# First mixer: one sink addition and one reciprocal for both steps of a pair, statistics side by side

## The chip, the cores and the metric

The kernel runs on one core of one Trainium2 chip. The metric is the device time of one execution in microseconds (us), taken as the median of repeated runs.

## The reference

The kernel computes two transformer blocks on 256 tokens of width 1024, in float32. The first block is a mixer followed by a mixture of experts with 32 experts; the second has a pooling and latent-attention mixer, a recurrent mixer, two cross-attentions and two gated feed-forward layers. The change touches only the attention of the first mixer. It has two kinds of heads: 24 dilated heads in three groups of eight, whose three groups are merged by a softmax over their log-sums, and 16 sliding-window heads with a sink.

```
# dilated: per group, then merged over the three groups
scores = q.k * hd**-0.5 + bias;  m = max;  p = exp(scores - m);  denom = sum(p)
out = (p @ v) / denom;  lse = m + log(denom)
alpha = softmax(lses over the 3 groups);  y = sum(alpha * outs)
# sliding window, with a sink per head
m = maximum(max(scores), sink);  p = exp(scores - m)
denom = sum(p) + exp(sink - m);  out = (p @ v) / denom
```

Merging three softmaxes by their log-sums equals one softmax over the three groups' scores side by side, and the kernel computes it so.

## The kernel before

The tokens are two blocks of 128. All weights come in units of 1 MB (128 partitions x 2048 elements); ScalarE makes the rounded high part of a unit (`whi`, L1653) and VectorE the remainder (`wlo`, L2337), and TensorE multiplies with high and low parts three times over. The DMAs of the units are issued by SyncE as buffers come free.

The attention of the first mixer has 32 steps (`steps_a`). Steps 0 to 15 are dilated (`dil`): one head index, one block of queries, the scores of the three groups side by side, so that a step has 3 x 128 scores per query for the first block and 3 x 256 for the second. Steps 16 to 31 are sliding-window (`swa`): two heads at a time, 2 x 128 or 2 x 256 scores. Steps are handled in 16 pairs; this document calls them pair 0 to pair 15. In the dilated part, pairs 0, 2, 4, 6 are two steps of 128 keys and pairs 1, 3, 5, 7 two steps of 256 keys. In the sink part (pairs 8 to 15) the first step of a pair has 128 keys, the second 256.

What each engine does, in the order of its program (`attend_two` of each):

- TensorE, for pair p: the scores of pair p+1 (`score_two`, L914), the transposes of the first step's probabilities (`turn`, L864), a quarter of a gate unit of the projection (`fourth_unit`, 12 matmuls, L701 to L703), the transposes of the second step, another quarter, then probabilities times values of both steps (`mix_two`, L937). The second `turn` waits until ScalarE has copied the first step's transposes out of PSUM.
- ScalarE: copies the transposes of both steps (`copy_turned`, L1766 and, for six blocks, L1769), then exponentials with their sums for both steps of the next pair (`exps`: L1751 dilated; L1747 for the two sinks and L1755 twice in the sink part). The sum arrives with the row called ACTIVATION_READ_ACCUMULATOR. After the exponentials of some pairs it makes a `whi` (L1653) or copies a finished gate unit out (L1724).
- VectorE: `probs` of the first step, `probs` of the second, the copy of a finished output (L2573), then for the next pair twice `bias_max` (the biased scores, L2500; their maximum, L2505 or L2508; with sinks L2510; the negated maximum, L2513 or L2515). After every odd pair's `bias_max` of the next pair it has one `wlo` to make (L2337), or at two places a shorter operation.

`probs` waits for the step's exponentials (`att_exp`), adds the sink's exponential to the sum (L2523, sink part only), takes the reciprocal (L2524) and scales the probabilities (L2526 for a dilated step, L2534 twice for a sink step). The small operations are chained: `link` puts a semaphore increment on one and makes VectorE wait for it before the next.

The scores lie in three buffers `S[s % 3]` of the scratch `scr`, the statistics of a step in the row `s % 3` of `sm` (columns 0 to 2 maxima, 3 to 5 negated, 6 to 8 sums, 9 to 11 reciprocals, 12 to 14 sinks' exponentials).

Of the kernel before, what the change touches and what calls it, by code (L numbers as in the profile page):

```python
# [24 lines left out]
ALU = mybir.AluOpType  # L25
ACT = mybir.ActivationFunctionType
AX = mybir.AxisListType
# [90 lines left out]
def build(nc, t, out):  # L118

    with ExitStack() as ctx:  # L120
# [28 lines left out]
        sm = sb("sm", [P, 3, 24])  # L149
# [73 lines left out]
        def tok_of(part):  # L223
# [39 lines left out]
        att_scored, att_biased, att_max, att_exp, att_probs = (sem("att_scored"), sem("att_biased"), sem("att_max"),  # L263
                                                               sem("att_exp"), sem("att_probs"))
# [129 lines left out]
        def score_bank(step, g):  # L394

            if step["kind"] == "dil":
                bank, at = 5 * step["head"], g * T
                if step["nk"] == P:
                    bank, at = step["head"], g * P
                elif g == 2:  # L400
                    bank, at = 1, step["head"] * T
            else:
                bank, at = g, step["qt"] * T if step["kind"] == "swa" else 0
                if step["kind"] in ("xa", "mla"):
                    bank, at = step["qt"], g * step["nk"]
            return ps[:, bank, at:at + step["nk"]]

        def gather_bank(c, low):

# [81 lines left out]
        S = [scr[:, b * 768:(b + 1) * 768].rearrange("p (g k) -> p g k", g=3) for b in range(3)]  # L491
# [16 lines left out]
        steps_a = attention("dil") + attention("swa")  # L508
# [1134 lines left out]
        def _(act):  # L1643
# [96 lines left out]

            def exps(s, step):
                act.wait_ge(att_max, s + 1)
                b, nk = s % 3, step["nk"]
                n = len(step["scores"])
                if step["sink"] is not None:
                    for g in range(2):
                        nc.scalar.activation(sm[:, b, 12 + g:13 + g],  # L1747
                                             sink_row[:, step["sink"] + g:step["sink"] + g + 1],
                                             ACT.Exp, bias=sm[:, b, 3 + g:4 + g])
                if step["merged"]:  # L1750
                    last = nc.scalar.activation(S[b][:, 0:n, 0:nk], S[b][:, 0:n, 0:nk], ACT.Exp,  # L1751
                                                bias=sm[:, b, 3:4], scale=step["scale"], accum_out=sm[:, b, 6:7])
                else:
                    for g in range(n):
                        last = nc.scalar.activation(S[b][:, g, 0:nk], S[b][:, g, 0:nk], ACT.Exp,  # L1755
                                                    bias=sm[:, b, 3 + g:4 + g], scale=step["scale"],
                                                    accum_out=sm[:, b, 6 + g:7 + g])
                last.then_inc(att_exp, 1)

            def copy_turned(s, step, PT):  # L1760
# [274 lines left out]
            for k, u in enumerate(u_br):  # L2035
                for half in range(2):
                    act.wait_ge(sg_scaled, 2 * k + half + 1)
                    two = sg[:, 8 * half + 2 * k:8 * half + 2 * k + 2, :]
# [9 lines left out]
            for c in range(DC):  # L2048
                last = nc.scalar.activation(xg[:, c, :], x[:, c, :], ACT.Copy, scale=vcol("g_ffn", c))
# [11 lines left out]
            for b in range(4):  # L2061
                last = nc.scalar.activation(tok_of(xh)[:, b, :, :], ps[:, b, :].rearrange("p (q k) -> p k q", k=4),
                                            ACT.Copy, scale=rcol[:, b // 2:b // 2 + 1])
# [10 lines left out]
            for b in range(2):  # L2074
                last = nc.scalar.activation(mem_sq[:, 4 * b:4 * b + 4, :], mem[:, 4 * b:4 * b + 4, :], ACT.Square)
# [245 lines left out]
        def _(dve):  # L2321
# [3 lines left out]
            def link(ins):  # L2325

                st["chain"] += 1
                ins.then_inc(dve_step, 1)
                dve.wait_ge(dve_step, st["chain"])
# [154 lines left out]
            def bias_max(s, step):  # L2484
                dve.wait_ge(att_scored, s + 1)
                if s >= 3:
                    dve.wait_ge(att_turned, s - 2)
                b, nk, n = s % 3, step["nk"], len(step["scores"])
                for g in range(n):
                    src = score_bank(step, g)  # L2490
                    dst = S[b][:, g, 0:nk]
                    if step.get("by_key"):
                        last = v.tensor_tensor(dst, src, mem_rstd, ALU.mult)
                    elif step["bias"] is None:
                        last = v.tensor_copy(dst, src)
                    elif step["bias"] == "causal":
                        last = v.tensor_tensor(dst, src, causal[:, T - nk:T], ALU.add)
                    else:
                        pi, slope = step["bias"][g]
                        last = v.scalar_tensor_tensor(out=dst, in0=pat[:, pi, T - nk:T], scalar=-slope, in1=src,  # L2500
                                                      op0=ALU.mult, op1=ALU.add)
                last.then_inc(att_biased, 1)
                dve.wait_ge(att_biased, s + 1)
                if step["merged"]:
                    link(v.tensor_reduce(sm[:, b, 0:1], S[b][:, 0:n, 0:nk], AX.XY, ALU.max))  # L2505
                    n = 1
                else:
                    link(v.tensor_reduce(sm[:, b, 0:n], S[b][:, 0:n, 0:nk], AX.X, ALU.max))  # L2508
                if step["sink"] is not None:
                    link(v.scalar_tensor_tensor(out=sm[:, b, 0:n], in0=sm[:, b, 0:n], scalar=step["scale"],  # L2510
                                                in1=sink_row[:, step["sink"]:step["sink"] + n],
                                                op0=ALU.mult, op1=ALU.max))
                    v.tensor_scalar(sm[:, b, 3:3 + n], sm[:, b, 0:n], -1.0, None, ALU.mult).then_inc(att_max, 1)  # L2513
                else:
                    v.tensor_scalar(sm[:, b, 3:3 + n], sm[:, b, 0:n], -step["scale"], None,  # L2515
                                    ALU.mult).then_inc(att_max, 1)

            def probs(s, step):
                dve.wait_ge(att_exp, s + 1)
                b, nk, n = s % 3, step["nk"], len(step["scores"])  # L2520
                k = 1 if step["merged"] else n
                if step["sink"] is not None:
                    link(v.tensor_tensor(sm[:, b, 6:6 + k], sm[:, b, 6:6 + k], sm[:, b, 12:12 + k], ALU.add))  # L2523
                link(v.reciprocal(sm[:, b, 9:9 + k], sm[:, b, 6:6 + k]))  # L2524
                if step["merged"]:
                    last = v.tensor_scalar(S[b][:, 0:n, 0:nk], S[b][:, 0:n, 0:nk], sm[:, b, 9:10], None, ALU.mult)  # L2526
                else:
                    for g in range(n):
                        if step.get("by_key"):
                            last = v.scalar_tensor_tensor(out=S[b][:, g, 0:nk], in0=S[b][:, g, 0:nk],  # L2530
                                                          scalar=sm[:, b, 9 + g:10 + g], in1=mem_rstd,
                                                          op0=ALU.mult, op1=ALU.mult)
                        else:
                            last = v.tensor_scalar(S[b][:, g, 0:nk], S[b][:, g, 0:nk], sm[:, b, 9 + g:10 + g], None,  # L2534
                                                   ALU.mult)
                last.then_inc(att_probs, 1)

            def attend(steps, y_of, between=None):
                base = st["step"]
# [27 lines left out]
            def attend_two(y_of, between):  # L2567
                n = len(steps_a)

                def out(s):  # L2570
                    if steps_a[s]["last"]:
                        dve.wait_ge(att_mixed, s + 1)
                        v.tensor_copy(y_of(st["y"], 1)[:, 0, :], ps[:, 4, 0:T]).then_inc(att_out, 1)  # L2573
                        st["y"] += 1

                bias_max(0, steps_a[0])
                bias_max(1, steps_a[1])
                for s in range(0, n, 2):
                    probs(s, steps_a[s])
                    probs(s + 1, steps_a[s + 1])  # L2580
                    if s:
                        out(s - 1)
                    if s + 2 < n:
                        bias_max(s + 2, steps_a[s + 2])
                        bias_max(s + 3, steps_a[s + 3])
                    between(s)
                    between(s + 1)
                out(n - 1)
                dve.wait_ge(att_out, st["y"])
                st["step"] += n  # L2590
# [850 lines left out]
```

## Time and profile before

| what | us |
|---|---|
| median of 3 runs (lowest to highest) | 1705.93 (1705.73 to 1707.23) |
| the profiled execution, its own time | 1706.17 |
| its span, first to last instruction | 1704.3 |
| TensorE matmul busy | 1635.1 (96%) |
| VectorE busy | 1328.5 (78%) |
| ScalarE busy | 1032.5 (61%) |
| attention of the first mixer | about 152 to 262 |

The busy shares are means over stages with different limits. An engine's rows come from one execution: each has a start and a duration, and in brackets the time the engine stood idle just before it and whose work ended that. The time of 1706.17 us contains the span and 1.87 us around it. A busy TensorE is not a TensorE at its peak, since the ends of matmuls are modelled.

### The profile page before, as it was taken

The numbers are of one execution on the slowest core, as the hardware profiler recorded it, in microseconds if no ns is written. First come the engines' busy times: TensorE is split into PE (matmuls) and PEld (weight loads), VectorE is DVE, ScalarE is ACT, GpSimd is POOL, SyncE is SP. The second block draws the span as 40 slices with busy tenths as digits, with TensorE's granted clock in tenths as the row PEclk, the third lists the DMA queues.
The fourth block names the chain that finished last, engine by engine and source line by source line (L and its number), as shares of the span: only waits on it lengthen the run. The fifth ranks groups of instructions, "written<-read, shape, count | busy, mean of one in ns | idle before, by whom it ended". The sixth has DMA issues, their size and how long they took to land.

```text
span 1704.3 us, 27827 instructions
## 1 busy us (share of the span) xinstructions
PE 1635.1 (96%) x10558; PEld 1429.4 (84%) x10558; DVE 1328.5 (78%) x1510; ACT 1032.5 (61%) x1137; POOL 60.8 (4%) x57
## 2 busy tenths in 40 slices
PE   8999989899999999999998988999999999999998
PEld 7998879778877667777776978999999999998887
DVE  6545897674589999999996987778767879677776
ACT  4333676454678999999986564454435394454443
POOL 0000000000000000000004230000000020000000
PEclk9998999999999999999999999999999999999999
DMA  9663124085799999999999443446554565445550
GB/s 324 195 191 100 54 72 152 9 321 182 256 370 422 422 423 422 423 422 423 423 418 336 135 151 110 138 149 222 187 183 150 172 199 181 140 139 196 192 177 25
DMA packets 186397, 392.21 MB, mean 230 GB/s; under 512 B 6976, under 2 KB 151104, under 8 KB 161728
## 3 DMA queue, kind: packets, MB, share of 16 engines
q1 hardware_dynamic: 184496, 383.89, 61.6%
q0 software_dynamic: 1808, 7.05, 1.1%
q8 instruction: 63, 1.03, 0.2%
q14 instruction: 30, 0.25, 0.0%
HBM read 380.29 MB, written 10.62 MB: 229 GB/s over the span
## 4 chain that ended last, share of the span: by engine, by line
PE 64%; DMA 13%; DVE 13%; issue 5%; ACT 4%; POOL 0%; SPq 0%; DVEq 0%; ACTq 0%; POOLq 0%
DMA raw<-w_e_up_dram 11%; PE ps L969 9%; DVE wlo L2337 6%; PE ps L683 5%; PE ps L688 5%; PE ps L684 5%; PE ps L975 5%; PE ps L1155 4%; PE ps L984 4%; PE ps L1104 3%; PE ps L1110 3%; PE ps L1106 2%; PE ps L777 1%; PE ps L773 1%; PE ps L771 1%
## 5 line engine op out<-in xcount | busy, mean ns | idle before, releaser
L2337 DVE TENSOR_TENSOR wlo<-raw,whi 128x2048 fp32r<-128x2048 f32 (+3 forms) x358 | 811.3, 2278 | 165.5 <-ACT whi L1653 157.2
L1653 ACT ACTIVATE whi<-raw 128x2048 fp32r<-128x2048 f32 (+3 forms) x358 | 675.7, 1891 | 301.8 <-PE ps L975 113.6
L683 PE MATMUL ps<-xh,whi 128*128 128x256 f32 x688 | 169.9, 287 | 3.2 <-DVE xl L2350 2.0
L684 PE MATMUL ps<-xl,whi 128*128 128x256 f32 x688 | 167.5, 283 | 0.0
L1104 PE MATMUL ps<-whi,xh 128*128 128x512 f32 x528 | 160.2, 396 | 0.0
L969 PE MATMUL ps<-xb,whi 128*128 128x512 f32 x672 | 160.2, 390 | 0.0
L1110 PE MATMUL ps<-wlo,xh 128*128 128x512 f32 x528 | 143.6, 396 | 2.6 <-DVE wlo L2337 2.4
L969 PEld LDWEIGHTS ps<-xb,whi 128*128 128x128 f32 x672 | 124.0, 188 | 24.4
L683 PEld LDWEIGHTS ps<-xh,whi 128*128 128x128 f32 x688 | 132.3, 192 | 4.3 <-issue 1.8
L684 PEld LDWEIGHTS ps<-xl,whi 128*128 128x128 f32 x688 | 132.3, 192 | 0.3
L1110 PEld LDWEIGHTS ps<-wlo,xh 128*128 128x128 f32 x528 | 97.0, 188 | 31.9 <-DVE wlo L2337 12.2
L1104 PEld LDWEIGHTS ps<-whi,xh 128*128 128x128 f32 x528 | 97.4, 188 | 20.4
L688 PE MATMUL ps<-xh,wlo 128*128 128x256 f32 x688 | 90.0, 283 | 0.0
L975 PEld LDWEIGHTS ps<-xb,wlo 128*128 128x128 f32 x672 | 86.2, 191 | 3.3
L975 PE MATMUL ps<-xb,wlo 128*128 128x256 f32 x672 | 87.2, 283 | 0.0
L688 PEld LDWEIGHTS ps<-xh,wlo 128*128 128x128 f32 x688 | 85.9, 192 | 0.0
L1155 PE MATMUL ps<-whi,ah 128*64 128x512 f32 (+1 forms) x280 | 74.9, 393 | 6.1 <-issue 2.8
L1155 PE MATMUL ps<-wlo,ah 128*64 128x512 f32 (+1 forms) x280 | 76.0, 397 | 2.1 <-DVE wlo L2337 0.3
L1155 PE MATMUL ps<-whi,al 128*64 128x512 f32 (+1 forms) x280 | 74.6, 392 | 0.0
L1155 PEld LDWEIGHTS ps<-wlo,ah 128*64 128x64 f32 (+1 forms) x280 | 39.9, 150 | 31.6 <-DVE wlo L2337 14.0
L1155 PEld LDWEIGHTS ps<-whi,ah 128*64 128x64 f32 (+1 forms) x280 | 41.3, 149 | 28.8 <-issue 7.4
L1681 ACT ACTIVATE xb<-x,vec 128x256 fp32r<-128x256 f32 x40 | 18.2, 502 | 70.5 <-DVE x L2469 70.5
(491 smaller groups left out, 3078.0 us busy)
## 6 DMA issues: line engine op xcount, KB each, us to landing
raw<-w_e_gate_dram SPq DMA_DIRECT2D x64, 1024.0 KB, 10.6
raw<-w_e_up_dram SPq DMA_DIRECT2D x64, 1024.0 KB, 10.5
raw<-w_e_down_dram SPq DMA_DIRECT2D x64, 1024.0 KB, 10.5
raw<-ffn_w_gate_up_dram SPq DMA_DIRECT2D x44, 1024.0 KB, 5.1
raw<-w_in_dram SPq DMA_DIRECT2D x30, 1024.0 KB, 5.5
raw<-ffn_w_down_dram SPq DMA_DIRECT2D x22, 1024.0 KB, 4.8
raw<-xa_w_kv_dram SPq DMA_DIRECT2D x16, 1024.0 KB, 5.5
raw<-xa_w_q_dram SPq DMA_DIRECT2D x8, 1024.0 KB, 5.0
```

The costliest lines, as they stand in the source:

```text
L683: nc.tensor.matmul(o[b], wh, h, start=b == 0 and a == 0, stop=False, skip_group_check=True)
L684: nc.tensor.matmul(o[b], wh, l, start=False, stop=False, skip_group_check=True)
L688: mm = nc.tensor.matmul(o[b], wl, h, start=False, stop=b == len(blocks) - 1 and a == len(parts) - 1, skip_group_check=True)
L969: nc.tensor.matmul(ps[:, bank + b, :], wh[:, k, b * P:b * P + P], xb[:, k, :, :].rearrange("p a t -> p (a t)"), start=k == 0, stop=False, ...
L975: mm = nc.tensor.matmul(ps[:, bank + b, 0:T], wl[:, k, b * P:b * P + P], xb_h[:, k, :], start=False, stop=k == DC - 1, skip_group_check=True)
L984: mm = nc.tensor.matmul(o, part[:, 2 * (j % 2) + k, (bank // 2) * P:(bank // 2) * P + P], weights[:, k, cols], start=begin and n == 0, sto ...
L1104: nc.tensor.matmul(o, h[:, k, :], wh[:, k, :], start=part == 0 and k == 0, stop=False)
L1106: nc.tensor.matmul(o, l[:, k, :], wh[:, k, :], start=False, stop=False)
L1110: mm = nc.tensor.matmul(ps[:, s % 2 + 2 * up, :], rows[s][0][:, k, :], wl[:, k, :], start=False, stop=part == 1 and k == 3)
L1155: mm = nc.tensor.matmul(o, src[s % 2][:, 2 * half + k, 0:w], weights[:, k, cols], start=start and k == 0, stop=stop and k == 1)
L1653: nc.scalar.activation(whi[u % HL][:, 0:n], raw[u % RAW][:, 0:n], ACT.Copy).then_inc(hi_ready, 1)
L2337: v.tensor_tensor(wlo[u % HL][:, 0:n], raw[u % RAW][:, 0:n], whi[u % HL][:, 0:n].bitcast(F32), ALU.subtract).then_inc(lo_ready, 1)
```

## The change

In the 16 pairs, `probs` of the two steps is replaced by `probs_two`, which waits for the exponentials of both steps, then makes one sink addition (sink part) and one reciprocal for both, and then scales the probabilities of the first and of the second step as before. For this the statistics of the two steps must lie in neighbouring rows of `sm`, so for the dilated and sink steps the row is `s % 2` and no longer `s % 3`. The later attentions keep `s % 3` and `probs`. The score buffers stay `S[s % 3]`.

```diff
+        def stat_slot(s, step):
+            return s % 2 if step["kind"] in ("dil", "swa") else s % 3
...
             def exps(s, step):
                 act.wait_ge(att_max, s + 1)
-                b, nk = s % 3, step["nk"]
+                b, nk, st_at = s % 3, step["nk"], stat_slot(s, step)
...
+            def probs_two(s):
+
+                two = steps_a[s:s + 2]
+                n = len(two[0]["scores"])
+                k = 1 if two[0]["merged"] else n
+                dve.wait_ge(att_exp, s + 2)
+                if two[0]["sink"] is not None:
+                    link(v.tensor_tensor(sm[:, 0:2, 6:6 + k], sm[:, 0:2, 6:6 + k], sm[:, 0:2, 12:12 + k], ALU.add))
+                link(v.reciprocal(sm[:, 0:2, 9:9 + k], sm[:, 0:2, 6:6 + k]))
+                for a, step in enumerate(two):
+                    b, nk = (s + a) % 3, step["nk"]
+                    if k == 1:
+                        last = v.tensor_scalar(S[b][:, 0:n, 0:nk], S[b][:, 0:n, 0:nk], sm[:, a, 9:10], None, ALU.mult)
+                    else:
+                        for g in range(n):
+                            last = v.tensor_scalar(S[b][:, g, 0:nk], S[b][:, g, 0:nk], sm[:, a, 9 + g:10 + g], None,
+                                                   ALU.mult)
+                    last.then_inc(att_probs, 1)
...
                 for s in range(0, n, 2):
-                    probs(s, steps_a[s])
-                    probs(s + 1, steps_a[s + 1])
+                    probs_two(s)
                     if s:
                         out(s - 1)
```

In `exps` and `bias_max` every `sm[:, b, ...]` becomes `sm[:, st_at, ...]`; nothing else changes there.

## Rows read from the trace of the kernel before

A "pair" here is the pair of steps whose probabilities or transposes the row belongs to; L1747 rows 215.26, 221.42 and 222.56 open the exponentials of the pair after the one whose transposes were just copied.

**Rows 1.** Page of the whole kernel, the chain that ended last, shares by engine

```profile
PE 64%; DMA 13%; DVE 13%; issue 5%; ACT 4%; POOL 0%; SPq 0%; DVEq 0%; ACTq 0%; POOLq 0%
```

**Rows 2.** VectorE waits in 152 to 262: line waited for, us, times, longest

```profile
DVE sm L2523 <- ACT scr L1755: 2.1, 3, 0.7
```

**Rows 3.** Timeline of VectorE, pairs 5, 6: start us, duration us, instruction [idle before]

```profile
191.75 0.17 DVE L2524 RECIPROCAL sm<-sm 128x1 f32<-128x1 f32 x1 [0.37 <-ACT scr L1751]
191.96 0.62 DVE L2526 TENSOR_SCALAR scr<-scr,sm 128x768 f32<-128x768 f32 x1
192.49 0.68 DVE L2500 SCALAR_TENSOR_TENSOR scr<-c,ps 128x128 f32<-128x128 f32 x3
...
199.70 1.08 DVE L2500 SCALAR_TENSOR_TENSOR scr<-c,ps 128x256 f32<-128x256 f32 x3 [0.65 <-PE ps L914]
```

**Rows 4.** Timeline of ScalarE, pair 5

```profile
191.53 0.19 ACT L1751 ACTIVATION_READ_ACCUMULATOR scr<-scr,sm 128x1 f32 x1
...
193.43 0.57 ACT L1766 ACTIVATE x<-ps 128x512 f32<-128x512 f32 x1
```

**Rows 5.** Timeline of TensorE, pair 5

```profile
191.44 0.87 PE L864 MATMUL ps<-c,scr 128*128 128x128 f32 x6
...
194.42 0.84 PE L864 MATMUL ps<-c,scr 128*128 128x128 f32 x6 [0.68 <-ACT x L1769]
...
196.62 1.53 PE L937 MATMUL ps<-x,arena 128*64 128x128 f32 x24
```

**Rows 6.** Timeline of VectorE, pairs 9 and 10

```profile
218.08 0.16 DVE L2523 TENSOR_TENSOR sm<-sm 128x2 f32<-128x2 f32 x1 [0.67 <-ACT scr L1755]
...
218.48 0.62 DVE L2534 TENSOR_SCALAR scr<-scr,sm 128x256 f32<-128x256 f32 x2
219.01 0.42 DVE L2573 COPY arena<-ps 128x256 f32<-128x256 f32 x1
...
224.57 0.15 DVE L2523 TENSOR_TENSOR sm<-sm 128x2 f32<-128x2 f32 x1
...
224.96 0.48 DVE L2534 TENSOR_SCALAR scr<-scr,sm 128x128 f32<-128x128 f32 x2
225.36 0.15 DVE L2523 TENSOR_TENSOR sm<-sm 128x2 f32<-128x2 f32 x1
```

**Rows 7.** Timeline of ScalarE, pairs 8 to 10

```profile
211.95 0.19 ACT L1755 ACTIVATION_READ_ACCUMULATOR scr<-scr,sm 128x1 f32 x1
...
214.76 0.60 ACT L1766 ACTIVATE x<-ps 128x512 f32<-128x512 f32 x1 [1.47 <-PE ps L864]
215.26 0.47 ACT L1747 ACTIVATE sm<-rows,sm 128x1 f32<-128x1 f32 x2
...
221.42 0.47 ACT L1747 ACTIVATE sm<-rows,sm 128x1 f32<-128x1 f32 x2
...
222.56 0.47 ACT L1747 ACTIVATE sm<-rows,sm 128x1 f32<-128x1 f32 x2
...
223.83 0.19 ACT L1755 ACTIVATION_READ_ACCUMULATOR scr<-scr,sm 128x1 f32 x1
```

**Rows 8.** Timeline of TensorE: pairs 8, 10 and 15

```profile
212.43 0.44 PE L864 MATMUL ps<-c,scr 128*128 128x128 f32 x2
...
214.13 0.60 PE L864 MATMUL ps<-c,scr 128*128 128x128 f32 x4
...
225.50 0.44 PE L864 MATMUL ps<-c,scr 128*128 128x128 f32 x2 [1.52 <-DVE scr L2534]
...
259.03 0.63 PE L864 MATMUL ps<-c,scr 128*128 128x128 f32 x4 [1.01 <-ACT x L1766]
```

**Rows 9.** Stretches in us: length, busy us PE, PEld, DVE, ACT, POOL, PEclk, DMA

```profile
149.75:150.50 0.75, 0.00 (x0) 0.00 (x0) 0.75 (x3) 0.00 (x0) 0.00 (x0) 0.95 0.96 340
156.25:160.50 4.25, 4.24 (x19) 3.23 (x20) 3.13 (x10) 1.26 (x5) 0.00 (x0) 0.50 0.00 0
224.00:225.50 1.50, 0.00 (x0) 0.00 (x1) 1.43 (x6) 0.49 (x2) 0.00 (x0) 1.00 0.00 0
```

More of the change, by code:

```diff
@@ L1746, in exps @@
                     for g in range(2):
-                        nc.scalar.activation(sm[:, b, 12 + g:13 + g],
+                        nc.scalar.activation(sm[:, st_at, 12 + g:13 + g],
                                              sink_row[:, step["sink"] + g:step["sink"] + g + 1],
-                                             ACT.Exp, bias=sm[:, b, 3 + g:4 + g])
+                                             ACT.Exp, bias=sm[:, st_at, 3 + g:4 + g])
                 if step["merged"]:
                     last = nc.scalar.activation(S[b][:, 0:n, 0:nk], S[b][:, 0:n, 0:nk], ACT.Exp,
-                                                bias=sm[:, b, 3:4], scale=step["scale"], accum_out=sm[:, b, 6:7])
+                                                bias=sm[:, st_at, 3:4], scale=step["scale"], accum_out=sm[:, st_at, 6:7])
                 else:
@@ L1755, in exps @@
                         last = nc.scalar.activation(S[b][:, g, 0:nk], S[b][:, g, 0:nk], ACT.Exp,
-                                                    bias=sm[:, b, 3 + g:4 + g], scale=step["scale"],
-                                                    accum_out=sm[:, b, 6 + g:7 + g])
+                                                    bias=sm[:, st_at, 3 + g:4 + g], scale=step["scale"],
+                                                    accum_out=sm[:, st_at, 6 + g:7 + g])
                 last.then_inc(att_exp, 1)
@@ L2488, in bias_max @@
                 b, nk, n = s % 3, step["nk"], len(step["scores"])
+                st_at = stat_slot(s, step)
                 for g in range(n):
@@ L2504, in bias_max @@
                 if step["merged"]:
-                    link(v.tensor_reduce(sm[:, b, 0:1], S[b][:, 0:n, 0:nk], AX.XY, ALU.max))
+                    link(v.tensor_reduce(sm[:, st_at, 0:1], S[b][:, 0:n, 0:nk], AX.XY, ALU.max))
                     n = 1
                 else:
-                    link(v.tensor_reduce(sm[:, b, 0:n], S[b][:, 0:n, 0:nk], AX.X, ALU.max))
+                    link(v.tensor_reduce(sm[:, st_at, 0:n], S[b][:, 0:n, 0:nk], AX.X, ALU.max))
                 if step["sink"] is not None:
-                    link(v.scalar_tensor_tensor(out=sm[:, b, 0:n], in0=sm[:, b, 0:n], scalar=step["scale"],
+                    link(v.scalar_tensor_tensor(out=sm[:, st_at, 0:n], in0=sm[:, st_at, 0:n], scalar=step["scale"],
                                                 in1=sink_row[:, step["sink"]:step["sink"] + n],
                                                 op0=ALU.mult, op1=ALU.max))
-                    v.tensor_scalar(sm[:, b, 3:3 + n], sm[:, b, 0:n], -1.0, None, ALU.mult).then_inc(att_max, 1)
+                    v.tensor_scalar(sm[:, st_at, 3:3 + n], sm[:, st_at, 0:n], -1.0, None, ALU.mult).then_inc(att_max, 1)
                 else:
-                    v.tensor_scalar(sm[:, b, 3:3 + n], sm[:, b, 0:n], -step["scale"], None,
+                    v.tensor_scalar(sm[:, st_at, 3:3 + n], sm[:, st_at, 0:n], -step["scale"], None,
                                     ALU.mult).then_inc(att_max, 1)
```

## Prediction

> **What bounds the kernel now.** I read the page first: of the chain that ended last TensorE has 64%, VectorE and the DMAs 13% each [rows 1]. That is a mean over the whole kernel. The change acts in one stretch, from about 152 to 262 us, so I then read that stretch engine by engine, and of each pair asked which wait ends last.
>
> In the dilated part the answer alternates. In a 256-key pair VectorE gets to the second step's reciprocal before ScalarE has its exponentials ready: it stands idle 0.37 us until 191.75 [rows 3]. The same row is there for pairs 1, 3 and 7. TensorE does not wait for that: it began the first step's transposes at 191.44, before the second step's exponentials were done at 191.53 + 0.19 = 191.72 [rows 4, 5]. What ends last there is ScalarE's copy of the first transposes (from 193.43, held up by a `whi` before it), for which TensorE waits 0.68 us with the second transposes [rows 4, 5]. In a 128-key pair VectorE has finished early and waits 0.65 us for TensorE's scores (199.70) [rows 3]. So in the whole dilated part saved VectorE time is not on the path.
>
> In the sink part VectorE works almost without a gap, and there its time counts; but in pairs 9, 11 and 15 it waits for the second step's exponentials, 2.1 us in all, at most 0.7 [rows 2]. In pair 10 TensorE waits 1.52 us for the first scaled probabilities (225.50) [rows 8].
>
> **The change, edit by edit.** Removed: 16 reciprocals and 8 sink additions of VectorE. Each costs its pitch, not its width: two of them take 218.08 to 218.48, so 0.20 each [rows 6]; a reciprocal in the dilated part 191.75 to 191.96, 0.21 [rows 3]. In sum 24 x 0.20 = 4.8 us of VectorE.
>
> Added: the first step's reciprocal now waits for the second step's exponentials. Queued behind that wait on VectorE are the scaling of the first step, of the second, the output copy and the next pair's biased scores; waiting for the first scaling are TensorE's first transposes and through them ScalarE's copy.
>
> Merged operations: no row shows one over 2 rows of statistics. The low end is the price of one operation (0.20), the high end that of two (0.40). One element and two elements per partition both have a pitch of 0.20 to 0.21 [rows 3, 6], so I take 0.20. 20 of them are on the path found below (4 dilated, 16 sink), so the high end would add 4 us. I give that end little weight; it would need a cost that no row shows for twice the elements.
>
> The row index `s % 2` for `s % 3`: no cost; a row of statistics is rewritten only by `bias_max` behind `probs_two` on the same engine. No DMA is moved, and no queue of SyncE or GpSimd is passed; the loads of weight units follow `wlo` and move with it.
>
> **Pair 0 and the 128-key pairs 2, 4, 6: nothing.** The exponentials of both steps are ready when VectorE comes, it gets 0.2 us earlier to a point where it waits 0.65 us for TensorE [rows 3]. That wait is the cover; nothing is gained or lost.
>
> **The 256-key pairs 1, 3, 5, 7: each a loss.** Let E be the end of the second exponentials, 191.72 in pair 5. Before, the second transposes began at 194.42, E + 2.70 [rows 5]. After: reciprocal at E + 0.03, first scaling 0.21 later, taking 0.62 [rows 3], and about 0.05 to TensorE (the pair-10 gap of 224.96 + 0.48 to 225.50 is 0.06 [rows 6, 8]): first transposes at E + 0.91. Transposes and a quarter unit take 194.42 to 196.62 = 2.20 [rows 5], so the second transposes begin at E + 3.11. The old wait for ScalarE's copy (0.68 us) is covered, since the copy can start almost as early as before. Loss 0.41 each. VectorE leaves the pair at E + 1.31 in place of 192.49 = E + 0.77 [rows 3]; the 0.65 us of wait in the next pair takes that up. From the second transposes on the chain runs through TensorE to the next pair's scores, so nothing gives it back: 4 x 0.41 = 1.64 us.
>
> **Pair 8: a loss.** E is 211.95 + 0.19 = 212.14 [rows 7]. After: addition at 212.18, two pitches of 0.20, scaling 0.48 [rows 6], 0.06 to TensorE: transposes at 213.12 in place of 212.43 [rows 8], 0.69 later, and TensorE is the chain from there.
>
> **Pairs 9 to 15: loss and gain nearly cancel.** Before, from the second transposes of pair 8 (214.13) to those of pair 15 (259.03) are 44.90 us [rows 8]. After, a pair is set by the longer of two loops:
> - through ScalarE: transposes to copy 0.63 (214.13 to 214.76), copy to exponentials 0.50, first step's 1.14 (221.42 to 222.56), second step's 1.46 (222.56 to 223.83 + 0.19) [rows 7, 8]; then 0.03 to VectorE, 0.40, 0.48, 0.06, and first to second transposes 1.70 (212.43 to 214.13) [rows 6, 8]. Sum 6.40.
> - through VectorE, where a `wlo` lies in between: addition and reciprocal 0.40, first scaling's pitch 0.40 (224.96 to 225.36), second scaling to copy 0.53, copy to the next addition 5.56 (219.01 to 224.57) [rows 6]. Sum 6.89. It holds for pairs 10 and 12; in 14 the operations in that place are shorter and the first loop holds.
>
> 5 x 6.40 + 2 x 6.89 = 45.78, against 44.90: loss 0.88. In the first loop VectorE's own release of the second exponentials comes only about 0.1 us sooner than ScalarE, so a small error there does not change it.
>
> Sum: 1.64 + 0.69 + 0.88 = 3.2 us. After 262 us TensorE's work follows at once, then routing, then expert loads that wait for the routing result; all of it moves along. On the profiled execution's 1706.17 this makes 1709.4; on the median of the runs, which is 0.24 lower, 1709.1.
>
> **Rivals.**
> (a) *The saving comes through.* If the second exponentials were always ready when VectorE comes, all 24 pitches would fall off a VectorE-bound path: -4.8 us, 1701.1. For it: the sink part is VectorE-bound, and behind a `wlo` (pair 10) both are ready. It decides from the point where E lies ahead of VectorE's arrival; in pairs 5 and 9 it lies behind it, by waits of 0.37 and 0.67 us even at the second step [rows 3, 6]. Against it also: the 0.65 us waits of the dilated part. This is also what the Trainium skill would have one expect: "VectorE: DVE Perf Modes", section on the TRN2 errata, says that each SBUF-source operation pays a fixed extra latency and that many small tiles should be made into fewer. The trace agrees on the fixed price, but not that it lies on the path.
> (b) *Partly hidden.* ScalarE or TensorE have more slack than the walk gives them, or the lost time is made up where VectorE is last; between -2 and +2.5 us, middle +1: 1706.9.
> (c) *The clock.* TensorE's wait before the last pair's first transposes grows: from the second transposes of pair 14 to there are 6.40 - 1.70 = 4.70 us, of which its work fills 2.20 and about half of a 24-matmul mix of 1.53 [rows 5], leaving some 1.7 us idle. After an idle 0.75 us the granted clock fell near 150 us, and while TensorE was busy from 156.25 it stayed at half (1.2 GHz) for 4.25 us; but 1.5 us of idle at 224 left it at 2.4 GHz [rows 9]. A fall would cost half of 4.25, 2.1 us: 1711.2.
> (d) *The merged operation costs as two:* +4 us more, 1713.1.
>
> **How the numbers follow.** This kernel's runs differ by about 0.1%, and 0.2% (3.4 us) is about what a measurement tells from no change; the forecast of +3.2 lies just inside. Chances: the walk as forecast (+2.5 to +4.2) 0.62, of which 0.36 below 3.4 and 0.26 above; (a) 0.06; (b) 0.15; (c) 0.14; (d) 0.03. Faster 0.06; same 0.36 + 0.15 = 0.51; slower 0.26 + 0.14 + 0.03 = 0.43. The range reaches from the middle of (b) to just past (c): 1706.8 to 1711.6, leaving out (a), (d) and the lower part of (b), less than 2 in 10.
>
> **What would show it.** In the trace of after: the first transposes of 256-key pairs 0.9 us behind the second exponentials' end; the time from one such pair to the next longer by 0.4; the second transposes of pairs 9, 11, 13, 14, 15 at 6.4 us from the ones before; VectorE busy 24 operations less, its idle time more by more than they took; the stretch from 262 us on unchanged in length. Wrong it would be if TensorE's first transposes did not move in pairs 1, 3, 5, 7, or if the merged operations had a pitch well over 0.20.

## The result and the profile after

| what | before | after |
|---|---|---|
| median, us (runs) | 1705.78 (9) | 1711.27 (9) |
| lowest to highest | 1705.03 to 1707.38 | 1704.97 to 1712.99 |
| profiled execution, its own time | 1706.17 | 1710.99 |
| its span | 1704.3 | 1709.1 |
| VectorE busy, instructions | 1328.5, 1510 | 1324.3, 1486 |

The changed kernel takes 1.0028 of the time before (95% interval 1.002 to 1.0036): 4.8 us more by this ratio; the two medians lie 5.5 apart. 24 VectorE instructions and 4.2 us of VectorE work are gone, and the kernel is slower. The predicted 1709.1 lies 2.2 under the median of 1711.27, which is inside the range of 1706.8 to 1711.6.

VectorE's timeline of pairs 5 and 6 after the change (start us, duration us, instruction, idle before it), the answer to [rows 3]:

```profile
193.01 0.17 DVE L2551 RECIPROCAL sm<-sm 128x2 f32<-128x2 f32 x1 [1.09 <-ACT scr L1755]
193.21 1.15 DVE L2555 TENSOR_SCALAR scr<-scr,sm 128x768 f32<-128x768 f32 x2
194.27 0.68 DVE L2505 SCALAR_TENSOR_TENSOR scr<-c,ps 128x128 f32<-128x128 f32 x3
...
201.27 1.08 DVE L2505 SCALAR_TENSOR_TENSOR scr<-c,ps 128x256 f32<-128x256 f32 x3 [0.63 <-PE ps L918]
```

ScalarE and TensorE beside it, for [rows 4, 5]:

```profile
192.79 0.19 ACT L1755 ACTIVATION_READ_ACCUMULATOR scr<-scr,sm 128x1 f32 x1
192.88 1.90 ACT L1657 ACTIVATE whi<-raw 128x2048 fp32r<-128x2048 f32 x1
194.80 0.60 ACT L1770 ACTIVATE x<-ps 128x512 f32<-128x512 f32 x1
```

```profile
193.89 0.87 PE L868 MATMUL ps<-c,scr 128*128 128x128 f32 x6 [1.12 <-DVE scr L2555]
...
196.03 0.82 PE L868 MATMUL ps<-c,scr 128*128 128x128 f32 x6
...
198.20 1.53 PE L941 MATMUL ps<-x,arena 128*64 128x128 f32 x24
```

VectorE's idle time at the reciprocal went from 0.37 to 1.09 us, and TensorE, which before started the first transposes while ScalarE was still at the second exponentials, now waits 1.12 us. The second exponentials end at 192.98; the first transposes start 0.91 after that. The next pair's wait for TensorE (0.65 before, 0.63 now) swallows whatever VectorE saved.

VectorE's timeline of pairs 9 and 10, for [rows 6]:

```profile
220.48 0.16 DVE L2550 TENSOR_TENSOR sm<-sm 128x4 f32<-128x4 f32 x1 [1.64 <-ACT scr L1759]
220.68 0.18 DVE L2551 RECIPROCAL sm<-sm 128x4 f32<-128x4 f32 x1
220.90 1.01 DVE L2558 TENSOR_SCALAR scr<-scr,sm 128x128 f32<-128x128 f32 x4
221.82 0.41 DVE L2597 COPY arena<-ps 128x256 f32<-128x256 f32 x1
...
227.38 0.16 DVE L2550 TENSOR_TENSOR sm<-sm 128x4 f32<-128x4 f32 x1
```

TensorE's transposes of pairs 8, 9 and 15, for [rows 8]:

```profile
215.02 0.44 PE L868 MATMUL ps<-c,scr 128*128 128x128 f32 x2 [0.64 <-DVE scr L2558]
...
216.73 0.60 PE L868 MATMUL ps<-c,scr 128*128 128x128 f32 x4
...
223.13 0.60 PE L868 MATMUL ps<-c,scr 128*128 128x128 f32 x4
```

```profile
260.85 0.44 PE L868 MATMUL ps<-c,scr 128*128 128x128 f32 x2 [1.86 <-DVE scr L2558]
...
262.55 0.60 PE L868 MATMUL ps<-c,scr 128*128 128x128 f32 x4
```

From the second transposes of pair 8 to those of pair 9 are 6.40 us, and from pair 8 to pair 15 45.82; the forecast had 6.40 and 45.78. VectorE's waits in the stretch, by line (us, times, longest), for [rows 2]:

```profile
DVE sm L2550 <- ACT scr L1759: 6.6, 6, 1.6
DVE sm L2551 <- ACT scr L1755: 5.2, 5, 1.1
DVE scr L2505 <- PE ps L918: 4.1, 5, 1.8
```

Before, beside the 2.1 us of [rows 2], the dilated part had

```profile
DVE sm L2524 <- ACT scr L1751: 1.7, 5, 0.4
```

The waits for the exponentials were 3.8 us in 8 places and are now 11.8 us in 11. VectorE has 4 us less to do and waits 8 us longer for them.

**Where the 4.8 us of the two traces lie.** I cut both at three marks that every kernel here has: VectorE's copy just before the attention (151.97 before, 152.61 after), its last output copy (261.94, 265.43), and the last of its conversions ahead of the first expert (`xc_l`, 355.79, 360.16). Up to the first mark the executions differ by 0.64, the attention by 2.85 (109.97 and 112.82), projection and routing by 0.88 (93.85 and 94.73), the rest by 0.4. The first two marks, before and after:

```profile
151.97 0.42 DVE L2870 COPY x<-ps 128x256 f32<-128x256 f32 x1 [1.29 <-PE ps L1266]
...
261.94 0.42 DVE L2573 COPY arena<-ps 128x256 f32<-128x256 f32 x1 [1.00 <-PE ps L937]
```

```profile
152.61 0.42 DVE L2893 COPY x<-ps 128x256 f32<-128x256 f32 x1 [1.29 <-PE ps L1270]
...
265.43 0.42 DVE L2597 COPY arena<-ps 128x256 f32<-128x256 f32 x1 [1.44 <-PE ps L941]
```

So the attention is 2.85 us longer, with the clock alike at its start; the rest of the difference is not in the lines that were changed.

### The profile page after: what moved, and what is told of

It reads as the page before. It is cut to its first block, busy times and chain, and to the rows that moved or that the text cites. A ratio compares the mean times of both kernels' runs of the same rounds, so it can differ in the third digit from the quotient of the medians.

```text
span 1709.1 us, 27803 instructions
## 1 busy us (share of the span) xinstructions
PE 1635.8 (96%) x10558; PEld 1429.5 (84%) x10558; DVE 1324.3 (77%) x1486; ACT 1031.9 (60%) x1137; POOL 60.9 (4%) x57
## 4 chain that ended last, share of the span: by engine, by line
PE 63%; DMA 14%; DVE 13%; issue 5%; ACT 4%; POOL 0%; SPq 0%; DVEq 0%; ACTq 0%; POOLq 0%
DMA raw<-w_e_up_dram 12%; PE ps L973 9%; DVE wlo L2341 6%; PE ps L687 5%; PE ps L692 5%; PE ps L688 5%; PE ps L979 5%; PE ps L1159 4%; PE ps L988 4%; PE ps L1108 3%; PE ps L1114 3%; PE ps L1110 2%; PE ps L781 1%; PE ps L777 1%; PE ps L775 1%
## 5 line engine op out<-in xcount | busy, mean ns | idle before, releaser
L973 PEld LDWEIGHTS ps<-xb,whi 128*128 128x128 f32 x672 | 124.0, 188 | 24.4
L1159 PEld LDWEIGHTS ps<-wlo,ah 128*64 128x64 f32 (+1 forms) x280 | 39.9, 150 | 31.3 <-DVE wlo L2341 13.7
```

Of the source, the lines that this page charges most:

```text
L973: nc.tensor.matmul(ps[:, bank + b, :], wh[:, k, b * P:b * P + P], xb[:, k, :, :].rearrange("p a t -> p (a t)"), start=k == 0, stop=False, ...
L1159: mm = nc.tensor.matmul(o, src[s % 2][:, 2 * half + k, 0:w], weights[:, k, cols], start=start and k == 0, stop=stop and k == 1)
```

## The experiments

The expectations speak of four theories. W: the wait for the second exponentials moves the path, and the walk of the prediction gives the time. C: what comes on top is time that TensorE spends at half clock in the routing stage. F: what comes on top is fixed and the same in each execution. K: what comes on top is falls of the clock inside the attention, because TensorE idles longer there.

In the table "attention" is the time between the first two marks in the one profiled execution; "half clock" is the time at the lower clock, from each execution's mean granted clock and span, as a mean over all executions of the kernel. The kernel before has 37.3 us of it (91 executions, standard error 0.7); by sets of runs 35.5 (beside after_again, wait_only, shift_27 and negated_sinks), 37.5 (beside the filled and the halved kernels) and 38.3 (beside the last four of the table), with standard errors of 1.0 to 1.2. The means in the table have standard errors of 0.7 to 3.6; the granted clock is recorded to 0.001, which is 3.4 us of half clock, so that small differences between them say little. The clock is at half for 10.2 us or 6.8 us in the first pairs, whichever the execution meets; with 10.2 an untouched attention takes 109.97 (before), with 6.8 it takes 109.33 to 109.39 (shift_27 and route_filled below). Changes of the attention are given against the one that fits.

| kernel | ratio of time to before (95%) | in us | attention | its change | half clock |
|---|---|---|---|---|---|
| after, first set | 1.0028 (1.002 to 1.0036) | +4.8 | 112.82 | +2.85 | 42.5 |
| after_again | 1.0025 (1.0013 to 1.0038) | +4.3 | 112.42 | +3.0 | 36.5 |
| wait_only | 1.0042 (1.0027 to 1.0056) | +7.2 | 117.42 | +8.1 | 43.2 |
| shift_27 | 1.0011 (1.0002 to 1.002) | +1.9 | 109.33 | 0 | 32.6 |
| negated_sinks | 0.9996 (0.9987 to 1.0005) | -0.7 | 107.69 | -2.3 | 40.6 |
| after_filled | 1.0022 (1.0012 to 1.0032) | +3.8 | 112.21 | +2.8 | 36.7 |
| before_filled | 1.0011 (1.0002 to 1.0019) | +1.9 | 111.35 | +2.0 | 35.5 |
| sink_only | 1.0026 (1.0017 to 1.0036) | +4.4 | 113.12 | +3.15 | 44.4 |
| dil_only | 1.0012 (1.0001 to 1.0022) | +2.0 | 110.76 | +1.4 | 37.9 |
| route_filled | 0.9979 (0.997 to 0.9988) | -3.6 | 109.39 | 0 | 22.9 |
| after_route | 1.0006 (0.9997 to 1.0015) | +1.0 | 112.13 | +2.7 | 23.9 |
| negated_route | 0.9977 (0.9968 to 0.9986) | -3.9 | 107.02 | -2.4 | 25.9 |
| where_free | 0.9995 (0.9986 to 1.0004) | -0.9 | 109.40 | -0.6 | 36.1 |

### after_again: the changed kernel once more

No edit.

> The changed kernel itself, beside the kernel before on one chip. Theory W (the wait moves the path): the attention stretch, from VectorE's copy before it to its last output copy, is 2.8 to 2.9 us longer than before, again. What comes on top (the first comparison had about 5 in all) is then not in the attention: theory C (clock) says that it lies in the routing stage, between the attention and the first expert, where TensorE spends more of its time at half clock, and that it varies from execution to execution. A rival of C, theory F (fixed), says the extra 2 us is there in each execution and in another place. Time expected: 1708.6 to 1711.5.

The attention was 112.42 with the shorter start (3.0 over 109.4), and the half-clock time in the routing stage 10.2 us as in the trace of before, where the first trace of after had 13.7. The two traces of the same kernel differ by 2.8 us in span, of which 1.5 was there before the attention began. So part of what two traces differ by belongs to the execution and not to the kernel.

### wait_only: the wait without the merging

```diff
             def probs(s, step):
-                dve.wait_ge(att_exp, s + 1)
+                dve.wait_ge(att_exp, s + 2 if step["kind"] in ("dil", "swa") and s % 2 == 0 else s + 1)
```

> The kernel before, with one edit: the first step's statistics wait for the exponentials of both steps, nothing is merged. Theory W: the wait alone costs 0.3 in each 256-key pair (1.2), 0.7 in pair 8, and in pairs 9 to 15 the loop through VectorE grows, 5 x 6.70 + 2 x 7.28 = 48.1 against 44.9: attention +5.1 us, that is 2.2 more than the changed kernel. A rival, that the wait is free and the shape of the merged operations costs the time, expects 0 here.

The loops are there as worked out. VectorE's sink additions of pairs 8, 9 and 10:

```profile
212.29 0.16 DVE L2523 TENSOR_TENSOR sm<-sm 128x2 f32<-128x2 f32 x1 [0.48 <-ACT scr L1755]
...
218.98 0.16 DVE L2523 TENSOR_TENSOR sm<-sm 128x2 f32<-128x2 f32 x1 [1.53 <-ACT scr L1755]
...
226.27 0.15 DVE L2523 TENSOR_TENSOR sm<-sm 128x2 f32<-128x2 f32 x1
```

218.98 - 212.29 = 6.69 and 226.27 - 218.98 = 7.29, against 6.70 and 7.28 expected, and 6.40 and 6.89 in the changed kernel (TensorE's second transposes, and the additions 220.48 and 227.38 above). The attention grew by 8.1 and not by 5.1. The trace shows what the walk did not have: the clock fell three times inside it, each time in or just behind a wait of TensorE for scaled probabilities of 1.87 to 2.15 us (pairs 10, 12 and 15). The first of them, with the columns us, busy time of TensorE, its weight loads, VectorE, ScalarE, GpSimd, granted clock and DMA:

```profile
225.30:227.15 1.85, 0.03 (x2) 0.00 (x0) 1.78 (x6) 0.83 (x3) 0.00 (x0) 1.00 0.00 0
228.50:232.00 3.50, 3.50 (x19) 3.50 (x18) 2.71 (x10) 1.68 (x8) 0.00 (x0) 0.52 0.23 81
```

TensorE was idle for 1.85 us at 2.4 GHz, took up work at 227.19, and from about 228.5 on ran 3.5 us at half. So the wait is not free, it costs more than all of the change. Merging pays back 0.29 us in a loop of the first kind and 0.40 in one of the second, 5 x 0.29 + 2 x 0.40 = 2.2 us. The rival with costly merged operations falls: in the changed kernel they take 162 ns (addition) and 165 to 179 ns (reciprocal), against 157 and 157 to 166 before.

### dil_only and sink_only: the change in halves

```diff
-                    probs_two(s)
+                    if s < 16:          # sink_only: s >= 16
+                        probs_two(s)
+                    else:
+                        probs(s, steps_a[s])
+                        probs(s + 1, steps_a[s + 1])
```

with `probs` taking its statistics from the same slots, `s % 2`.

> Merged operations in pairs 0 to 7 only. Theory W: attention +1.2 us, four times 0.31 (the first transposes to the second took 2.10 us, not the 2.20 of the forecast). Theory K: TensorE's idle times there are 1.1 us among much work, the clock stays up, so the total moves by about 1.2 too.

> Merged operations in pairs 8 to 15 only. Theory W: attention +1.57 us (0.69 + 0.88). Theory K: the long idle times of TensorE are all in this part, so the total moves by more than 1.6, by 2.5 to 4.5.

The dilated half lengthens the attention by 1.4 (expected 1.2) and the total by 2.0. The sink half lengthens the total by 4.4 (2.9 to 6.1), within the 2.5 to 4.5 that theory K expected, and its attention by 3.15 where the walk has 1.57. The halves add up to more than the whole change (6.4 against 4.8, each with 1.6 to 1.8 us to either side), so the totals alone can't be divided between them. The sink half's trace has a fall of the clock in the last pair, after TensorE's longest wait:

```profile
259.04 0.44 PE L868 MATMUL ps<-c,scr 128*128 128x128 f32 x2 [1.88 <-DVE scr L2559]
...
261.48 1.06 PE L868 MATMUL ps<-c,scr 128*128 128x128 f32 x4
...
264.24 0.88 PE L941 MATMUL ps<-x,arena 128*64 128x128 f32 x12
```

```profile
259.00:260.00 1.00, 0.96 (x8) 0.97 (x9) 0.95 (x4) 1.00 (x2) 0.00 (x0) 0.89 0.00 0
260.00:261.00 1.00, 1.00 (x6) 1.00 (x6) 1.00 (x1) 0.12 (x1) 0.00 (x0) 0.50 0.00 0
```

First to second transposes took 2.44 for 1.70, second transposes to mix 2.76 for 1.96 (262.55 to 264.51 in the changed kernel): 1.5 us, which is the excess. The changed kernel waits equally long there (1.86 us before 260.85), but in its profiled execution the clock held, and so it did behind the same wait in after_again (1.88) and after_route (1.86):

```profile
259.00:260.85 1.85, 0.00 (x1) 0.00 (x1) 0.88 (x5) 1.85 (x5) 0.00 (x0) 1.00 0.00 0
```

### after_filled and before_filled: no idle TensorE in the attention

```diff
             def turn(s, step):
-                pe.wait_ge(att_probs, s + 1)
                 if s >= 1:
                     pe.wait_ge(att_pt, s)
+                for _ in range(counts.get(s, 0)):
+                    nc.tensor.transpose(ps[:, 2, 0:P], ident, ident)
+                pe.wait_ge(att_probs, s + 1)
```

`counts` stands for the numbers written out in the edit, by step: 2 to 15 in after_filled, 3 to 12 in before_filled, there also before some second transposes.

> The changed kernel with spare transposes of 128 x 128 on TensorE in its waits of the attention (2 to 15 before the first transposes of a pair, each set shorter than the wait it fills), so that TensorE is hardly idle there. Theory K: in many executions of the changed kernel the clock falls inside the attention, because TensorE idles up to 1.9 us at a time; with the waits filled this is gone, the attention takes 2.85 us more than before as in the walk, and the median comes down by 1 to 2.5 us from the changed kernel's, to 1708 to 1710, with less spread. Theory W alone (the walk, no clock in it) and the rival that the rest lies in the routing stage expect the median of the changed kernel, within 0.5 us.

> The kernel before with its own waits of TensorE in the attention filled in the same way (3 to 12 transposes). The control: before, the idle times are shorter (1.5 us at most, one or two of them). Theory K: within 0.7 us of the kernel before. If the filling did something else, it would show here too.

after_filled came to a median of 1710.42 and a mean 1.2 us (standard error 0.8) under that of the changed kernel; its half-clock time is that of the kernel before. The direction is the one expected, but the median missed the 1708 to 1710 and the difference is not out of the noise: inconclusive by itself. The control was badly made: in before_filled the spare transposes were too long for the waits of second transposes, which came 0.3 to 0.7 us later behind the first ones than in route_filled, in pairs 3, 5, 7, 9, 11 and 15. Its attention grew by 2.0 us, which is as much as the 1.9 of its total.

### shift_27: a delay behind an untouched attention

```diff
             attend_two(PT_first, gates_between)
+            for _ in range(27):
+                nc.tensor.transpose(ps[:, 3, 0:P], ident, ident)
```

> The kernel before with 27 extra transposes of 128 x 128 on TensorE right behind the attention, into an unused bank: about 2.9 us of pure delay, the attention itself untouched. Theory C: the total moves by more or less than 2.9 (by 1 to 6), since the routing stage meets another phase of the clock's changes; its half-clock stretches differ from those of before. Theory F: exactly +2.9, 1708.7, the half-clock stretches as before.

The transposes took from 260.48 to 263.40, 2.9 us as meant. The total moved by 1.9 (0.3 to 3.4), which holds the fixed 2.9 too, so the ratio does not tell the theories apart. Its half-clock time of 32.6 us is 4.7 under that of all executions of before, but 2.9 (standard error 1.6) under those of its own set, and its trace has the same 10.2 us in the routing stage as before's. That a delay changes what the clock does later is not shown by this run.

### route_filled, after_route: the routing stage at full clock

```diff
             mm.then_inc(logits_turned, 1)
+            for _ in range(22):
+                nc.tensor.transpose(ps[:, 6, 0:P], ident, ident)
```

and likewise 8 behind `ranks_mm`, 2 behind `starts_mm` and 28 behind `order_mm`.

> The kernel before with spare transposes in TensorE's four waits of the routing stage (22, 8, 2 and 28, each set shorter than its wait at full clock), nothing else. Theory C (a part of the time is lost because the granted clock is at half in and behind that stage): half-clock time falls by some 10 us of the mean 37, and the time by 2 to 5 us, to 1701 to 1704. The rival, that the clock costs nothing there because other engines are last, expects no change or up to 1 us more, for the spare work.

> The changed kernel with the same spare transposes in the routing stage. With that stage's clock fixed in both, what is left between this and route_filled is the attention alone: the walk's 2.85 us, plus the clock's falls inside the attention (up to 1.5 us in the mean). Rival: the difference stays at the full 4.5 us that lie between the two kernels now.

The stretch 325 to 350 us in before, then in route_filled:

```profile
325.00:350.00 25.00, 16.01 (x81) 13.04 (x80) 20.01 (x70) 15.08 (x27) 2.80 (x4) 0.80 0.39 150
```

```profile
325.00:350.00 25.00, 22.10 (x143) 17.93 (x141) 20.71 (x68) 16.31 (x27) 2.24 (x3) 1.00 0.47 185
```

With 60 transposes that compute nothing the kernel is 3.6 us faster. Over all traces the time from the last output copy to the first expert follows the half-clock time in it: 92.38 us with none (route_filled, after_route), 93.26 to 93.85 with 10.2 (five traces without a delay), 94.73 with 13.7 (after), 95.27 with 17.1 (sink_only). Where the clock also fell near 300 us, in the projection, it is 1.4 us more: 93.82 with 3.4 there alone (negated_route), 96.64 to 96.67 with 20.5 in all (dil_only, wait_only, negated_sinks). TensorE's wait in that place is 1.60 us in all 14 traces, and the clock fell behind it in these four only. So theory C is right that the clock costs here. The traces do not place the whole 3.6 us: of the 3.8 between the spans of before and route_filled 1.5 lie in this stage, the rest in what differs between executions elsewhere.

That it explains the excess of the changed kernel is not borne out. With the clock at full in the routing stage of both, the changed attention still costs 1.0006 / 0.9979 = 1.0027, as before; the means differ by 4.6 us (standard error 0.75). The attentions of the two traces differ by 2.74, projection and routing not at all, the mean half-clock times by only 1 us (standard error 1.4). And the 12 executions of after_route fall into two groups at nearly the same half-clock time (means of 23.1 and 24.4 us): five from 1704.8 to 1705.8, which is 1.7 to 2.7 us over the mean of route_filled where the attention has 2.7 to 2.85, and seven from 1708.3 to 1710.6. The profiled one belongs to the lower group, so what happens in the upper one no trace of this kernel shows.

One kept trace has a loss that is neither in the attention nor at half clock. From the third mark to VectorE's last `scr<-ps,scr` operation in the experts, after_filled took 550.56 us (356.77 to 907.33) and after_again 548.84 (357.36 to 906.20); the other traces have 548.66 to 549.22, but where_free 549.70. Of the 1.7 us, 1.3 arise within 20 us near 490, where ScalarE waits for a DMA that stores expert results. That operation, and ScalarE's wait in 479 to 503 (478 to 502), in after_again and then in after_filled, both at a granted clock of 1.00 from 357 to 906:

```profile
906.20 0.42 DVE L2638 TENSOR_TENSOR scr<-ps,scr 128x256 f32<-128x256 f32 x1 [1.09 <-ACT scr L1834]
ACT arena L1844 <- DMA compact_y<-arena: 2.1, 1, 2.1
```

```profile
907.33 0.42 DVE L2640 TENSOR_TENSOR scr<-ps,scr 128x256 f32<-128x256 f32 x1 [0.97 <-ACT scr L1836]
ACT arena L1846 <- DMA compact_y<-arena: 3.5, 1, 3.5
```

So one execution's experts took 1.7 us longer with the clock the same. Whether this happens more often behind the changed attention, and makes the upper group, no run tested.

### negated_sinks, negated_route: small operations taken away without a wait

```diff
...
-                    link(v.scalar_tensor_tensor(out=sm[:, b, 0:n], in0=sm[:, b, 0:n], scalar=step["scale"],
-                                                in1=sink_row[:, step["sink"]:step["sink"] + n],
-                                                op0=ALU.mult, op1=ALU.max))
-                    v.tensor_scalar(sm[:, b, 3:3 + n], sm[:, b, 0:n], -1.0, None, ALU.mult).then_inc(att_max, 1)
+                    v.scalar_tensor_tensor(out=sm[:, b, 3:3 + n], in0=sm[:, b, 0:n], scalar=-step["scale"],
+                                           in1=neg_sinks[:, step["sink"]:step["sink"] + n],
+                                           op0=ALU.mult, op1=ALU.min).then_inc(att_max, 1)
...
```

`neg_sinks`, the row of negated sinks, is made once ahead of the attention. negated_route has this edit and that of route_filled.

> The kernel before with the negation of the maxima folded into the operation before it in the sink part (a row of negated sinks is made once): 16 small VectorE operations fewer, and no wait added. Theory W (a small operation is worth its 0.20 us where VectorE is last and nothing new is waited for): attention 1.5 to 3 us shorter, time 1703 to 1704.5. A rival, that small operations are hidden everywhere in this stretch, expects no change.

> The folded negation together with the filled routing stage. If the folded negation really saves 2.3 us in the attention and only the clock took it back, this lies 2 to 2.5 us under route_filled and 4 to 7 us under the kernel before: 1699 to 1702. If the saving is not real, it equals route_filled.

The attention lost 2.3 and 2.4 us; 1.5 to 3 was expected. In negated_sinks, VectorE's rows ahead of pair 10 show the maximum, one operation, and the next work at once:

```profile
221.76 0.69 DVE L2509 TENSOR_REDUCE sm<-scr 128x2 f32<-128x512 f32 x1
222.49 0.16 DVE L2511 SCALAR_TENSOR_TENSOR sm<-sm,neg_sinks 128x2 f32<-128x2 f32 x1
222.56 2.29 DVE L2338 TENSOR_TENSOR wlo<-raw,whi 128x2048 fp32r<-128x2048 f32 x1
```

16 operations of 0.20 are 3.2 us, of which 2.3 came through. But the totals did not follow. negated_sinks was expected at 1703 to 1704.5 and came to 1706.24, within the noise of before. It has 5.1 us (standard error 1.6) more at half clock than before in its own set, and its trace shows where the gain went: 17.1 us at half clock in the routing stage and a fall near 298, and from the last output copy to the first expert 96.67 us where before took 93.85. negated_route has a mean 0.4 us (standard error 0.4) under that of route_filled, not 2 to 2.5. In the two traces its attention is 2.4 us shorter and the stretch from the last output copy to the first expert 1.4 longer (93.82 and 92.38), with a fall near 296, where TensorE waits for the projection's inputs; another 1.0 was lost before the first mark and behind the third. In the mean its half-clock time is 3.0 us longer, with a standard error of 2.1. negated_route is the fastest of all, 0.9977 of before, but it owes this to the filled routing stage. Two of its twelve executions took 3650 and 4400 us and are left out of its mean; their cause is not known.

### where_free: merged only where both are ready

```diff
-                    probs_two(s)
+                    if s in (4, 8, 12, 20, 24):
+                        probs_two(s)
+                    else:
+                        probs(s, steps_a[s])
+                        probs(s + 1, steps_a[s + 1])
```

> Merged operations only in pairs 2, 4, 6, 10 and 12, where both exponentials are ready when VectorE comes. Theory W: nothing from pairs 2, 4 and 6, about 0.2 us each from 10 and 12 (0.4 off VectorE, of which ScalarE's chain passes on half): attention 0.4 us shorter than before, no pair longer, the time within 0.2% of before. Rival: merging costs by itself, then the attention is longer.

Pair 10, VectorE:

```profile
225.28 0.16 DVE L2551 TENSOR_TENSOR sm<-sm 128x4 f32<-128x4 f32 x1
225.47 0.18 DVE L2552 RECIPROCAL sm<-sm 128x4 f32<-128x4 f32 x1
225.69 1.01 DVE L2559 TENSOR_SCALAR scr<-scr,sm 128x128 f32<-128x128 f32 x4
```

There is no wait before the addition, and the attention is 0.6 us shorter than before (0.4 was expected), by one trace against one. Since this kernel has the statistics at `s % 2` in all pairs, the changed row index costs nothing either. The same edit gains where the later of its two inputs is early, and loses where it is late. The time does not show it.

## Why the prediction was right or wrong

- *The 128-key pairs give nothing:* right. The wait for TensorE's scores is 0.63 us after, 0.65 before.
- *The 256-key pairs lose 0.41 each:* right in mechanism, a little large. The first transposes come E + 0.91, as forecast, the second E + 3.05 in place of E + 3.11, since first to second took 2.14 (193.89 to 196.03) and not the 2.20 taken from the neighbouring stretch. From the scores of pair 5 to those of pair 7 the time grew from 13.49 (186.21 to 199.70) to 13.80 (187.47 to 201.27): 0.31.
- *Pair 8 loses 0.69:* right. Exponentials end at 214.04, first transposes start at 215.02, 0.98 later; 212.14 + 0.98 = 213.12 was the forecast's.
- *Pairs 9 to 15, 45.78 for 44.90:* right, 45.82.
- *Merged operations at 0.20:* right; 220.48 to 220.68 to 220.90 are 0.20 and 0.22. Rival (d) is out.
- *Sum 3.2:* the attention grew by 2.85, which is the forecast less the 0.4 of the 256-key pairs.
- *All of it moves along, so the total is 3.2 more:* this step was mis-sized. The total grew by 4.8 (3.4 to 6.1), and the stretch behind 262 us, which was to stay the same, was 1.3 longer in the first trace (0.9 of it up to the first expert, with 3.4 us more at half clock) and in after_again 93.85 up to the first expert, as before. What makes up the excess stays open. Rival (c), a fall of the clock behind TensorE's longer wait, is shown for wait_only and sink_only, at a price of 1.5 us in the latter (2.1 was forecast), but in none of the three traces of the changed attention that have that wait. The mean half-clock time of the changed kernel, 40.1 us over 15 executions against 37.3 before, would allow at most 1.4 us, and the difference of 2.8 has a standard error of 2.0. Between after_route and route_filled, where the routing stage is at full clock in both, some 1.3 us (standard error 0.75) are left over the walk and the clock.
- *The range:* that the median of 1711.27 lies inside is in part luck. It is 0.3 us below the upper end, which was set by (c) and not by the walk. The lower end was called the middle of (b), but the middle of -2 to +2.5 is +0.25 and not +1.
- *Rival (a), that the saving comes through:* out. VectorE's arrival before the exponentials decided it, as the rows said. The Trainium skill's rule on many small operations ("VectorE: DVE Perf Modes", the section on the TRN2 errata) holds for the operations: 16 fewer, without a new wait, made the attention 2.3 us shorter. It says nothing of the wait that came with this merging.
- *Faster, same, slower at 0.06, 0.51, 0.43:* the ratio's interval of 1.002 to 1.0036 begins at the bound of 0.2%, so the outcome is slower, which had 0.43, and not the likeliest of the three; the forecast of +3.2 itself lay just under the bound.

## What to carry to other kernels

Two small operations on the results of two steps may be merged where the later result is there anyhow; elsewhere the first step's consumer pays for the wait. Wait and merging can be priced apart from the rows: here, by the walk, 5.1 us of wait against 2.2 of merging. Where an operation can go without a new wait, as with the folded negation, most of its pitch comes off the path, here 2.3 of 3.2 us; but on a kernel this long a gain of 2 us can be lost again to the clock.

## What was not expected of the hardware

- Work that computes nothing moved the total about as much as the edits. 60 spare transposes in the routing stage took half-clock time from 38.3 (before, same set) to 22.9 us and the time to 0.9979 of before.
- With 2.3 us less in the attention (negated_sinks) the time at half clock was 40.6 us, with before at 35.5 in the same set. With 2.9 us of delay it was 32.6, which is not clear of the noise.
- In or just behind a wait of TensorE of 1.87 to 2.15 us the clock fell in wait_only (three times) and sink_only (once), and held behind 1.86 to 1.88 us in after, after_again and after_route. Behind 1.60 us near 300 us it fell in 4 of 14 traces; behind 1.49 to 1.54 us in pairs 10 and 12 it held in all nine traces that have these waits. From one execution alone it can't be said which will happen.
